# Attention bias on VectorE, gates with stationary weights, and vector lengths folded into exponents and the last norm

## The reference

```
delta = i + BLOCK - j
valid = (delta >= 0) & (delta <= n_back) & (kpos >= 0)
bias = -slopes[:, None, None] * (delta * stride)
s = jnp.where(valid[None, :, None], s + bias, -jnp.inf)
m = jnp.max(s, axis=-1, keepdims=True)
p = jnp.exp(s - m)
```

```
qkv = silu(causal_depthwise_conv(proj[..., :3 * GDN_WIDTH], conv_w))
q = l2norm(q) * GDN_HEAD_DIM ** -0.5
k = l2norm(k)
beta = sigmoid(b)
g = -exp(a_log) * softplus(a + dt_bias)
o = chunk_gated_delta_rule(q, k, v, g, beta)
o = rmsnorm(o, norm_g) * silu(z)
```

## Time and profile before

| | us |
|---|---|
| median of 3 runs | 3190.45 |
| lowest and highest | 3190.24, 3194.05 |
| the profiled execution | 3184.84 |
| its span | 3183.5 |
| mean granted clock of TensorE in it | 0.925 of full |

### The profile page before, as it was taken

The page is one execution under the profiler, slowest core; times in us unless marked ns, Lnnn a source line. Parts: engine busy times, 40 slices in busy tenths (PEclk is TensorE's granted clock), DMA queues, the critical chain, the costliest instruction groups (busy, mean ns, idle before and its releaser), DMA issues. The chain is left out here.

```text
span 3183.5 us, 35362 instructions
## 1 busy us (share of the span) xinstructions
PE 2773.0 (87%) x14088; PEld 2196.5 (69%) x14088; DVE 1217.3 (38%) x2129; ACT 841.5 (26%) x1646; POOL 528.8 (17%) x627
## 2 busy tenths in 40 slices
PE   6999968689869996699888999988779678889997
PEld 5898968466545553586666878766676576677886
DVE  5323143342231111302545666345445544343333
ACT  2323231332121111113553222233113112332222
POOL 3545354300012222200001000010220220100000
PEclk9999978799879998799898999989889889999998
DMA  6323310013249998210013666231003001232322
GB/s 214 106 97 102 106 40 26 11 37 89 66 159 403 420 414 316 79 41 20 1 33 99 186 185 192 70 84 40 1 1 80 1 1 43 67 98 82 109 78 68
DMA packets 325651, 339.40 MB, mean 107 GB/s; under 512 B 19120, under 2 KB 296752, under 8 KB 313072
## 3 DMA queue, kind: packets, MB, share of 16 engines
q1 hardware_dynamic: 303280, 280.21, 26.8%
q0 software_dynamic: 22208, 56.93, 5.0%
HBM read 370.63 MB, written 16.78 MB: 122 GB/s over the span
## 5 line engine op out<-in xcount | busy, mean ns | idle before, releaser
L332 DVE TENSOR_TENSOR sb_w_lo<-sb_weights,sb_w_hi 128x1024 fp32r<-128x1024 f32 (+2 forms) x215 | 239.8, 1124 | 505.6 <-ACT sb_w_hi L326 505.3
L374 PE MATMUL bank<-sb_h_hi,sb_w_hi 128*128 128x512 f32 x1040 | 422.2, 406 | 11.6 <-DVE sb_w_lo L332 11.6
L376 PE MATMUL bank<-sb_h_hi,sb_w_lo 128*128 128x512 f32 x1040 | 409.3, 394 | 0.0
L375 PE MATMUL bank<-sb_h_lo,sb_w_hi 128*128 128x512 f32 x1040 | 408.8, 393 | 0.0
L326 ACT CAST sb_w_hi<-sb_weights 128x1024 fp32r<-128x1024 f32 x224 | 215.5, 969 | 556.3 <-PE bank L376 492.1
L415 POOL TENSOR_TENSOR sb_scratch<-sb_scratch 128x512 f32<-128x512 f32 x30 | 38.6, 1287 | 1316.8 <-ACT sb_scratch L405 1316.8
L374 PEld LDWEIGHTS bank<-sb_h_hi,sb_w_hi 128*128 128x128 f32 x1040 | 197.1, 190 | 72.1 <-issue 30.1
L911 PE MATMUL bank<-sb_weights,sb_hT 128*128 128x256 f32 x960 | 233.2, 400 | 13.0 <-DVE sb_padded L1362 12.4
L911 PEld LDWEIGHTS bank<-sb_weights,sb_hT 128*128 128x128 f32 x960 | 213.9, 285 | 22.6 <-issue 13.2
L375 PEld LDWEIGHTS bank<-sb_h_lo,sb_w_hi 128*128 128x128 f32 x1040 | 197.3, 190 | 46.0 <-issue 5.3
L376 PEld LDWEIGHTS bank<-sb_h_hi,sb_w_lo 128*128 128x128 f32 x1040 | 197.0, 189 | 43.4
(11 more groups left out here) (478 smaller groups left out, 5090.9 us busy)
## 6 DMA issues: line engine op xcount, KB each, us to landing
sb_weights<-ffn_w_in SPq DMA_DIRECT2D x88, 512.0 KB, 3.9
sb_mod_weights<-ada_w POOLq DMA_DIRECT2D x24, 1024.0 KB, 5.7
sb_weights<-ada_w SPq DMA_DIRECT2D x24, 1024.0 KB, 5.2
sb_expert_weights<-w_down SPq DMA_DIRECT2D x17, 1024.0 KB, 9.3
sb_weights<-w_in SPq DMA_DIRECT2D x16, 1024.0 KB, 5.4
sb_weights<-ffn_w_out SPq DMA_DIRECT2D x32, 512.0 KB, 3.9
sb_weights<-gdn_w_in SPq DMA_DIRECT2D x32, 512.0 KB, 4.2
sb_expert_weights<-w_up SPq DMA_DIRECT2D x14, 1024.0 KB, 17.6
```

The source lines that it names most:

```text
L332: dve.tensor_tensor(u.lo[:, 0:u.kt, :], u.chunk.w, u.hi[:, 0:u.kt, :].bitcast(F32), ALU.subtract).then_inc(*k.lo.one())
L374: pe.matmul(bank[:], u.hi[:, kk, :], act[0][:, kk, :], start=first and kk == 0, stop=False)
L375: pe.matmul(bank[:], u.hi[:, kk, :], act[1][:, kk, :], start=False, stop=False)
L376: mm = pe.matmul(bank[:], u.lo[:, kk, :], act[0][:, kk, :], start=False, stop=last and kk == u.kt - 1)
```

## The change

**The bias.** The product L566 and the table of slopes are gone. DVE computes `distance * (-slope) + bank` in place in the bank, with a new semaphore `biased` between it and the reduction, and it is DVE that waits for the distances. All 8 modulation pieces of a group are now asked for in its projection (steps 6, 8, 11, 13, 16, 18, 21, 23), and none in its attention.

**The gates.** The 16 columns of gate weights are stationary and 512 tokens move: 24 matmuls into 16 rows. ACT copies the 16 rows out, PE transposes them in four pieces, and DVE adds `dt_bias` and negates b. The sigmoid becomes exp(-softplus(-b)), on the same Abs, Exp, Ln path as the other gate. The generators are advanced at other steps.

**The lengths.** q and k are no longer scaled. For q the sums of squares are kept in a row buffer and enter the root of the gated norm at the end, times epsilon. For k the sums are taken into columns by four one-column matmuls per head, the transposes of k and the copies stand in the channel loop, and `lengths_act` and `lengths_dve` compute k's inverse length as a logarithm and as a factor on 128x16 columns. The factor is multiplied into the gate columns; the logarithm is the bias of the chunk's second exponent, which becomes four activations of 128 columns with a bias column each.

```diff
@@ attention_pe
-            mm = pe.matmul(bank[:, 0:j.n], j.query, j.keys, start=True, stop=False)
+            mm = pe.matmul(bank[:, 0:j.n], j.query, j.keys, start=True, stop=not j.bias)
...
-        if s in mod:
-            modulation_pe(k, mod[s])
@@ attention_dve
             dve.wait_ge(*k.scored.at(s + 1))
+            if j.slope:
+                dist, slope = j.slope
+                dve.scalar_tensor_tensor(out=k.bank[s % 3][:, 0:j.n], in0=dist, scalar=-slope,
+                                         in1=k.bank[s % 3][:, 0:j.n], op0=ALU.mult, op1=ALU.add
+                                         ).then_inc(*k.biased.one())
+                dve.wait_ge(*k.biased.at(s + 1))
@@ dilated
-    k.nc.tensor.wait_ge(k.distances_in, 16)
+    k.nc.vector.wait_ge(k.distances_in, 16)
...
-        on_pe = {7 + 5 * n: p for n, p in enumerate(pieces[:4])}
+        on_pe = {6 + 5 * n // 2: p for n, p in enumerate(pieces)}
...
-        on_pe = {11 + 9 * n: p for n, p in enumerate(pieces[4:])}
-        attention_pe(k, jobs, True, False, on_pe)
+        attention_pe(k, jobs, True, False)
@@ gates_pe
+    for kk in range(KD):
+        for term, (a, b) in enumerate(((0, 0), (0, 1), (1, 0))):
+            mm = pe.matmul(bank[0:2 * H, :], gt.ab[a][:, kk, :], h[b][:, kk, :], start=kk == 0 and term == 0,
+                           stop=kk == KD - 1 and term == 2)
+    mm.then_inc(*k.projected.one())
+    yield
+    pe.wait_ge(*k.mixed_in.at(1))
     for i in range(NT):
-        for kk in range(KD):
-            for term, (a, b) in enumerate(((0, 0), (0, 1), (1, 0))):
-                mm = pe.matmul(bank[:, i * 2 * H:(i + 1) * 2 * H], h[a][:, kk, i * P:(i + 1) * P], gt.ab[b][:, kk, :],
-                               start=kk == 0 and term == 0, stop=kk == KD - 1 and term == 2)
+        mm = pe.transpose(bank[:, i * 2 * H:(i + 1) * 2 * H], k.scr[9][0:2 * H, i * P:(i + 1) * P],
+                          k.const("ident", 2 * H)[:, 0:2 * H])
@@ gates_act
-    act.activation(gt.beta, b3[:, :, H:], ACT.Sigmoid)
+    act.copy(k.scr[9][0:2 * H, :], k.bank[6][0:2 * H, :]).then_inc(*k.mixed_in.one())
+    yield
...
+    act.activation(gt.beta, gt.beta, ACT.Exp)
@@ channels_pe
-        if s in (1, 7):
+        if s in (1, 3, 6):
             next(other, None)
...
+            elif n < 2 * HG:
+                if n == HG:
+                    pe.wait_ge(*k.reduced.at(1))
                 for i in range(NT):
-                    mm = pe.transpose(k.bank[4 + n % 2][:, i * P:(i + 1) * P], block(acc, i), k.const("ident"))
+                    at = i * HG + n - HG
+                    mm = pe.matmul(k.bank[7][:, at:at + 1], block(acc, i), k.const("ones")[:, 0:1], start=True,
+                                   stop=True)
+                mm.then_inc(*k.summed.one())
+            if n >= HG:
+                src = k.heads[1][:, n - HG, :] if n < 2 * HG else acc
+                if n >= HG + 2:
+                    pe.wait_ge(*k.act_copied.at(n - HG - 1))
+                for i in range(NT):
+                    mm = pe.transpose(k.bank[4 + n % 2][:, i * P:(i + 1) * P], block(src, i), k.const("ident"))
@@ new
+def query_rows_dve(k, hg):
+    sums, rows = k.bank[7][0:8, :], k.scr[11][0:8, :]
+    dve.wait_ge(*k.summed.at(HG))
...
+def lengths_act(k, gt):
+    act.activation(flat(gt.ln), k.bank[7][:, 0:NT * HG], ACT.Ln, bias=k.eps[:, 0:1]).then_inc(*k.shifted.one())
+    act.wait_ge(*k.shifted.at(1))
+    act.activation(flat(gt.rk), flat(gt.ln), ACT.Exp, scale=-0.5).then_inc(*k.shifted.one())
...
+def lengths_dve(k, gt, hg):
+    dve.tensor_scalar(gt.lrk, gt.ln, -0.5, None, ALU.mult)
+    dve.wait_ge(*k.shifted.at(2))
+    for out, col in ((gt.bk, gt.beta), (gt.bek, gt.bexp), (gt.kd1, gt.kdec1), (gt.kd0, gt.kdec0)):
+        last = dve.tensor_tensor(out, col[:, :, hs], gt.rk, ALU.mult)
@@ chunk_act
-    act.activation(t.dec[:], t.dec[:], ACT.Exp).then_inc(*t.act.done(i, "dec"))
+    for hh in range(HG):
+        ex = act.activation(block(t.dec, hh), block(t.dec, hh), ACT.Exp, bias=gt.lrk[:, i, hh:hh + 1])
@@ delta_net
-        rows_invert_dve(k, rows)
-        normalise_pe(k, rows, kT)
-        normalise_act(k, ktok)
-        normalise_dve(k, (qT, kT))
```

195 lines of the change are left out of this document (88 added, 107 removed).

## The result

The changed kernel takes 3135.3 us (median of 4 runs, 3134.2 to 3138.5) against 3192.1 us before on the same chip: a ratio of 0.9824, 95% interval 0.9807 to 0.9841, or 57 us less. The forecast was 3149.5 us with a range of 3133 to 3173: the direction was right and the time lies inside the range, near its fast end; 41 us were forecast. The profiled executions differ by less, 3184.84 against 3136.05 us (spans 3183.5 and 3134.4).

What follows compares the result with a forecast made beforehand. TensorE, busy 2773.0 of 3183.5 us, was taken as the main bound. Attention -14.4, gates -6.6 and +2.1, lengths -22.1 total -41.0: 3184.84 becomes 3143.8, on the median 3149.5 us; range 3133 to 3173.

Steps and rivals of the forecast that it cites:

- Part A: Dilated attention and projections: bias moved from TensorE to DVE, modulation pieces all moved into the projections; -14.4 us.
- The bound of -24: Fast limit for the attention change: new DVE pass at the reduction's 0.29 and 0.42 us, no overhead; about -24 us.
- Cover: Projections: GpSimd's modulation pieces are ready before PE asks, DVE's longer overlap costs nothing; 12 more pieces cost +5.4 us.
- Part B: Delta net's gates and channel loop: cheaper gate matmuls, less half clock, added waits; -6.6 us first head group, +2.1 second.
- Part C: Lengths, from last channel product through the chunks: handover -12.85, chunks +1.8 us, each twice; -22.1 us in all.
- The lower bound of part C: Fast limit for the lengths, handover and chunks: chunks free of added cost; -28 us.
- the upper one: Slow limit for the lengths, handover and chunks: table switches at double price, chunks 2 us a tile; -12 us.
- Price twofold (1): Attention: new DVE pass costs double, DVE bounds all three groups, +9 us there; program 3173 us; chance 0.10.
- Longer waits (2): Gates, channel loop and chunks: longer waits, gates -1 and lengths -15 us; program 3162 us; chance 0.20.
- Clock (3): Attention: PE's idle time halves its granted clock, about +20 us there; program 3184 us, no difference; chance 0.04.
- Slower (4): Attention: DVE's wait-pass-wait-reduce chain takes 0.49 us more a job, 47 us; program 3197 us; chance 0.03.
- No waits and a cheap pass (5): No waits in the gates, attention's new DVE pass at 0.29 us; program 3133 us; chance 0.05.

## Why the prediction was right, and where its steps failed

- **The bound.** Right: the stages named became 52 us shorter in the profile, and the program 57 by the medians. That the time lies in the range is in part luck, since several terms were missed in the same direction.
- **Profile against median.** The forecast was made on a profile 5.6 us under the median, and the new runs put the median 7.3 us over it, while the changed kernel's profile is 0.7 over its own. The two experiments that kept the old attention took 416.3 and 416.6 us from the first projection's start to the end of the third attention, where the profile of before has 411.3. These 5 us are a third of what was missed (57 - 41 = 16): no term of the sum, but the execution that it was read from.
- **Part A, price of the pass.** The pass with its semaphore was taken at 0.37 us and measured at 0.32, of an operation of 288 ns; the lower bound, the reduction's row, was the true one and not the row of the same operation elsewhere (342). The time from job to job was right, 0.84 and 1.21 us for 0.87 and 1.21. Groups 1 and 2 still came out 1.9 and 1.8 us shorter than forecast: their first and last eight jobs go faster than the middle (0.73 and 0.77 us each), and the mean is 0.79. The bound of -24 does not come out of its own prices: 72 x 0.08 + 24 x 0.09 is 8, and gives -22.
- **Part A, what the bias and what the pieces bring.** The sum counted the stalls, the clock and the pieces' own matmuls as things that "leave" beside the bias. By the time they are most of it: 17.7 of 20.1 us, with 3.7 for the bias alone. In groups 1 and 2 the bias costs 1 us each (forecast 2.9); in group 0 it brings 9.2 on top of the pieces.
- **Part A, the projections.** Cover held: PE was not idle, +5.3 in all against +5.4.
- **Part B.** Right in its terms for the gates: 5.7 us of matmuls at full clock, waits of 1.86 and 2.58 us for 1.7 and 2.2, and 8.4 us measured alone for 8.75 (some 1.4 of it from the closer matmuls). Mis-sized is the +2.1 per head group for k's sums and transposes. In head group 1 the four products beside which they stand take 6.78, 6.74, 7.03 and 6.73 us for 6.62: +0.8 in all. And a term is missing: the 6 ns a matmul, 1.5 to 1.8 us in twelve products. Together they are the -0.7 that head group 1 gained. The 227 ns stand in every kernel with the new gates except the three with the early lengths, the 233 ns in those and in every kernel with the old gates; why is open. The reordered kernels add one small tile in SBUF, and the new gates have other tiles; whether the place of the tiles matters was not tested.
- **Part C.** The handover is 12.5 us for 11.3: the transposes of v ran at half clock (0.64 in that stretch) and copies waited for them. The chunks are the larger miss, -1.3 for +1.8 in each head group. Their first terms came true: the first exponent stands 0.36 us earlier (the table load of 1.28 is gone, matmuls at half clock take 0.9 of it), and from the first tile's to the second's, and from the third's to the fourth's, it is 0.65 and 0.64 us more. The gain is in the two long stretches behind the second and the fourth tile, 1.3 and 0.9 us, where PE's time at half clock fell from 11.3 to 6.9 and from 11.1 to 6.9 us. The sum had no term for the clock inside the chunks; that it is the cause is read from this side by side, and from the run with one exponent, whose last stretch has 11.4 us at half clock and is as long as before. The lower bound of part C is not borne out by its terms either: with the chunks free they give -25.7, not -28, and the prices named for the upper one (5.1 us more for the table loads, 16 for the chunks) give about -5, not -12.
- **Rivals.** Price twofold (1): no. Longer waits (2): no. Clock (3): not in the changed kernel (0.99 at 23.00 of 29.80 us busy), but near: 0.80 with the bias alone and 0.83 with one more operation on DVE. Slower (4): the semaphore costs 0.1 us, not 0.5. No waits and a cheap pass (5): the cheap pass came true, the waits stayed, and that the time is nearest to this one is luck.

The prediction weighed a rule that spoke against the change. Operations of 280 to 290 ns start 0.19 to 0.21 us after each other in the rows above, and 0.32 where one waits for the other. The Trainium skill, "VectorE: DVE Perf Modes", section The DRAIN you can't avoid, says that the next operation does not start until the pipe is empty, and adds that one that is not held starts earlier; the prediction left the second half out. The trace agrees with both: it shows the full length only for the pair with a semaphore between. The prediction also held that GpSimd could not hold up the new pass; the kernel with the bias alone bears that out (291 and 423 ns).

## What to carry to other kernels

Before a change is credited with a gain, undo its parts one at a time: here a rearrangement of side work on GpSimd, which the change made in passing, brought nearly five times what its headline edit brought alone (17.7 and 3.7 us). Where an experiment shows no difference in the time, look at the trace too: here one exponent for four was faster at each place it touched, and the granted clock took it back. If an engine stalls on a copy inside SBUF, look for GpSimd at work at that moment, and place such work where the vector engine has time. When a queue idles before its last item and has a row of small things after it, move the small things ahead, and fetch the next table with an activation on one column; here that made a handover 4.5 us shorter, and 5.6 with the copies moved too, of which a part was lost elsewhere.

## What the runs showed of the hardware that was not expected

- A scalar_tensor_tensor in place on a bank with its other input in SBUF takes 288 ns for 128 columns and 422 ns for 256, the same as a reduction that only reads the bank (291, 424). It is indifferent to GpSimd: 291 and 423 ns where GpSimd was busy for 35 of 38 us, while a copy of 64x512 within SBUF went from 424 to 1237 ns on the mean.
- PE held a granted clock of 0.99 over 29.8 us in which it was busy for 77%, with idle times between its jobs of at most 0.85 us. With one more operation on DVE it was busy for 76% of 35.3 us, with idle times of at most 0.95 us, and got 0.83; with stalls of 2.1 to 2.9 us between jobs it got 0.80.
- A sum over partitions by four one-column matmuls for each k head (0.95 us), with four transposes (0.63), in place of one sum matmul of 512 columns (1.02), made a head group's products 0.8 us longer; they were not free.
- The same fp32 product matmul of 512 columns follows the one before after 233 ns in some of these kernels and after 227 in others, always the same within a kernel in these stages. The cause is open.
